# A hybrid decoder layer on one core: the compressed attention's normalisation and the choice of blocks become two steps on VectorE

## The reference

```python
# for each block of 128 queries
s = q @ k_cmp.T * scale - slope * dist          # 63 compressed keys
p_cmp = softmax(masked s) * ok
o_cmp = p_cmp @ v_cmp
imp = (p_cmp summed over heads) @ overlap       # importance of 32 blocks
score = where(ok_sel, where(forced, 1e4, imp), -1)
idx = top_k(score, 4)                           # blocks chosen per token
o_sel = attention over the chosen blocks
o_win = attention over a window of 512
o_a = g0 * o_cmp + g1 * o_sel + g2 * o_win
...
merged = sigmoid(m0) * (o_a @ w_br_nsa) + sigmoid(m1) * (o_b @ w_br_s5)
       + sigmoid(m2) * (o_c @ w_br_sb)          # m0, m1, m2 = h @ columns of w_in
```

## Time and profile before

| | |
|---|---|
| median of three runs | 1378.1 us |
| the profiled execution: its time, its span | 1379.38 us, 1377.6 us |
| TensorE matmuls busy | 1314.1 us (95%) |
| VectorE, GpSimd, ScalarE busy | 795.0, 603.8, 517.6 us |
| chain that ended last: TensorE, VectorE | 87%, 7% of the span |

### The profile page before, as it was taken

The page is one execution under the profiler, slowest core; times in us unless marked ns, Lnnn a source line. Parts: engine busy times, 40 slices in busy tenths (PEclk is TensorE's granted clock), DMA queues, the critical chain, the costliest instruction groups (busy, mean ns, idle before and its releaser), DMA issues.

```text
span 1377.6 us, 18689 instructions
## 1 busy us (share of the span) xinstructions
PE 1314.1 (95%) x7157; PEld 1059.5 (77%) x7157; DVE 795.0 (58%) x1289; ACT 517.6 (38%) x990; POOL 603.8 (44%) x395
## 2 busy tenths in 40 slices
PE   6999898999999889999989999999999999999998
PEld 5888565789787667666778888878888888888887
DVE  5895676632625867667636341287444543479952
ACT  6322553400122255555511010265545554463441
POOL 4213003134542310111148746267776777757662
PEclk9999999999999989999999999999999999999999
DMA  7530100032201210000155524151222211156343
GB/s 195 49 56 20 46 1 19 29 63 58 59 20 39 86 45 9 24 24 5 45 181 191 202 94 181 39 176 46 88 77 74 62 54 54 47 185 199 115 113 146
DMA packets 143673, 110.75 MB, mean 80 GB/s; under 512 B 41936, under 2 KB 116048, under 8 KB 143568
## 3 DMA queue, kind: packets, MB, share of 16 engines
q1 hardware_dynamic: 142784, 107.98, 26.8%
q10 hardware_dynamic: 800, 1.57, 0.5%
HBM read 86.33 MB, written 21.63 MB: 78 GB/s over the span
## 4 chain that ended last, share of the span: by engine, by line
PE 87%; DVE 7%; ACT 3%; issue 2%; DMA 0%; SPq 0%; ACTq 0%; DVEq 0%
PE ps L964 24%; PE ps L966 23%; PE ps L965 23%; PE ps L1506 2%; PE ps L1490 2%; PE ps L1222 1%; PE ps L1239 1%; PE ps L1471 1%; PE ps L1252 1%; DVE merged L2304 1%; PE ps L1473 1%; DVE hTl L2062 1%; PE ps L1083 1%; PE ps L1422 1%; PE ps L1196 0%
## 5 line engine op out<-in xcount | busy, mean ns | idle before, releaser
L964 PE MATMUL ps<-hTh,wh 128*128 128x512 f32 x784 | 314.8, 402 | 3.1 <-DVE hTl L2062 2.3
L966 PE MATMUL ps<-hTh,wl 128*128 128x512 f32 x784 | 306.2, 391 | 0.0
L965 PE MATMUL ps<-hTl,wh 128*128 128x512 f32 x784 | 306.0, 390 | 0.0
L924 POOL TENSOR_TENSOR wl<-raw,wh 128x512 fp32r<-128x512 f32 x162 | 235.2, 1458 | 154.7 <-ACT wh L1901 154.7
L828 POOL TENSOR_TENSOR wh<-raw,zero 128x1280 fp32r<-128x1280 f32 (+2 forms) x36 | 79.9, 2220 | 474.1 <-PE ps L966 470.1
L964 PEld LDWEIGHTS ps<-hTh,wh 128*128 128x128 f32 x784 | 148.0, 189 | 38.1 <-issue 8.0
L831 POOL TENSOR_TENSOR wl<-raw,wh 128x1280 fp32r<-128x1280 f32 (+2 forms) x45 | 129.7, 2881 | 105.4 <-ACT wh L1661 102.6
L964 PE MATMUL ps<-wh,hTh 128*128 128x512 f32 (+2 forms) x496 | 173.1, 349 | 0.0
L966 PE MATMUL ps<-wh,hTl 128*128 128x512 f32 (+2 forms) x496 | 173.0, 349 | 0.0
L965 PE MATMUL ps<-wl,hTh 128*128 128x512 f32 (+2 forms) x496 | 172.8, 348 | 0.0
L966 PEld LDWEIGHTS ps<-hTh,wl 128*128 128x128 f32 x784 | 147.4, 188 | 32.1
(11 more groups left out here) (377 smaller groups left out, 2338.6 us busy)
## 6 DMA issues: line engine op xcount, KB each, us to landing
raw<-in_w_in SPq DMA_DIRECT2D x35, 512.0 KB, 3.9
raw<-in_w_up SPq DMA_DIRECT2D x64, 256.0 KB, 2.8
arena<-in_w_down SPq DMA_DIRECT2D x32, 256.0 KB, 3.7
v_down<-arena SPq DMA_DIRECT2D x32, 256.0 KB, 2.6
raw<-v_down SPq DMA_DIRECT2D x32, 256.0 KB, 2.7
raw<-in_w_down SPq DMA_DIRECT2D x24, 256.0 KB, 2.9
merged<-in_x SPq DMA_DIRECT2D x8, 512.0 KB, 6.5
raw<-in_w_out SPq DMA_DIRECT2D x8, 512.0 KB, 3.7
```

The costliest lines, as they stand in the source:

```text
L924: eng.tensor_tensor(wlf[:, w_slot(n)], raw_piece(n), whf[:, w_slot(n)].bitcast(F32), ALU.subtract).then_inc(S("fw_split"), 1)
L964: mm(out_, ah, bh, start=first, stop=False, skip_group_check=True)
L965: mm(out_, ah, bl, start=False, stop=False, skip_group_check=True)
L966: return mm(out_, al, bh, start=False, stop=last, skip_group_check=True)
```

## The change

Three things, all in the order of steps; no instruction is added or taken away.

- `select_blocks` is cut in two functions: `normalise` (to `pc_ready`) is what `soft` calls now, `select_blocks` (the rest) is the new step `select`.
- First half: `select` 0 stands three pieces later than `soft` 0, after piece 24, so that VectorE's merge (8, 0) comes between the two parts. Second half: `select` 1 stands after piece 49, so that both `ka` steps and merge (10, 1) come between.
- Second half on TensorE: `pc` 4 and `pc` 5 stand after piece 50 instead of 53, and `pvc` 4 to 6, `pc` 6 and 7 come three pieces sooner too; `pvc` 7 and `qa` 0 two, `mk` 1 and `qa` 1 one; on VectorE, `qa` 0 now comes ahead of merge (11, 0).

```diff
-        PLAN += F(13) + [("half", 0), ("half_exp", 0)] + F(14, 20) + [("split", 0)] + F(20, 22) + [("soft", 0)] + F(22, 37)
+        PLAN += F(13) + [("half", 0), ("half_exp", 0)] + F(14, 20) + [("split", 0)] + F(20, 22) + [("soft", 0)] + F(22, 25) + [("select", 0)] + F(25, 37)
...
-        PLAN += [("ka", 0), ("ka", 1)] + F(48, 51) + [("kb", 0), ("kb", 1)] + F(51, 54)
-        PLAN += [("pc", 4), ("pc", 5)] + F(54) + [("pvc", 4), ("pc", 6)] + F(55) + [("pvc", 5), ("pc", 7), ("qa", 0)] + F(56)
-        PLAN += [("pvc", 6), ("mk", 1), ("pvc", 7), ("qb", 0)] + F(57, 59) + [("qa", 1)] + F(59, 61) + [("qb", 1)]
+        PLAN += [("ka", 0), ("ka", 1)] + F(48, 50) + [("select", 1)] + F(50) + [("kb", 0), ("kb", 1), ("pc", 4), ("pc", 5)]
+        PLAN += F(51) + [("pvc", 4), ("pc", 6)] + F(52) + [("pvc", 5), ("pc", 7)] + F(53) + [("pvc", 6), ("qa", 0)] + F(54)
+        PLAN += [("pvc", 7), ("qb", 0)] + F(55) + [("mk", 1)] + F(56, 58) + [("qa", 1)] + F(58, 61) + [("qb", 1)]
...
-            def select_blocks(hb):
+            def normalise(hb):
...
                 ins.then_inc(S("pc_ready"), 1)
+
+            def select_blocks(hb):
+
                 then(tt(imp, php[:, :, 0:64:2], php[:, :, 2:66:2], ALU.add))
...
                 elif kind == "soft":
+                    normalise(n)
+                elif kind == "select":
                     select_blocks(n)
```

## The result

| | before | after |
|---|---|---|
| median, us | 1378.1 (5 runs, 1376.68 to 1379.85) | 1369.89 (5 runs, 1367.68 to 1372.0) |
| ratio to before | | 0.9936, 95% interval 0.9925 to 0.9947 |
| profiled execution: its time, its span | 1379.38, 1377.6 | 1367.76, 1366.0 |

The change makes the kernel 0.64% faster, some 8.8 us (7.3 to 10.3). The forecast was 1368.4 in a range from 1366.0 to 1373.0.

What follows compares the result with a forecast made beforehand. TensorE's matmuls were busy 95% of the span, so only its idle and low-clock time could be won. 3.4 + 6.2 = 9.6 us off 1379.38 gives 1369.8; off the median, less one tenth, 1368.4, range 1366.0 to 1373.0.

Steps and rivals of the forecast that it cites:

- the two waits: TensorE waits on L2301 before pieces 29 (2.80 us) and 54 (5.42 us), claimed to come from VectorE's order, not its speed.
- First half, 3.4 us: Moving select 0 behind merge (8, 0) wins 4.4 us at piece 29, less about 1.0 waited at piece 34.
- the race at the end of L828: On VectorE, whether L2473 or GpSimd's L831 starts first around 431.15: first half wins 4.4 or 3.4 us; 3.4 taken.
- rival 1: L2473 slips in ahead of L831 or isn't held: first half 4.4 us, total 10.6, so 1367.5; chance 0.27.
- the signs that the prediction named: In the first half's selection, L2472 lasts about 0.9 us and L2473 either 0.23 or about 3.
- Second half, 6.2 us: Wait before piece 54 (5.42 us) and its low clock (2.6) go, less a wait of 1.75 before pc 4.
- The new wait: In the second half, TensorE waits 1.75 us before pc 4 for pc_ready, ended by L2459, with no clock loss.
- the store: Third row of merged lands 3.8 us after L2304, at 479.4; ScalarE's qa 0 waits, TensorE keeps 4.9 us of cover.
- Rival 3: Something unseen sets the main loop's start, and the second half's gain is waited away: 3.4 us left, 1374.7; chance 0.08.
- Rival 4: A slow store landing delays qa 0 and merge (11, 0) behind it; a landing of 20 us gives 1380; chance 0.02.
- rival 2: The clock falls at piece 34, pc 4 or both, each costing up to 1.5 us: 1370 to 1371.5; chance 0.18.
- The shift is kept to the end: After 500 us nothing is bound to an absolute time, so the 9.6 us won should last to the end.

Runs made afterwards that it cites:

- pc_only: Changed kernel, but select 1 called right behind soft 1, TensorE's new order kept; mean 1370.9 us, ratio 0.9941 to the kernel before.
- first_only: Kernel before with only the first half changed (select 0 after piece 24); mean 1374.4 us, ratio 0.9967 to the kernel before.
- after_again: The changed kernel itself, timed once more without any edit; mean 1369.2 us.
- both: Changed kernel with select 0 after piece 29, and pc 4, 5 and what follows up to mk 1 one piece later; mean 1370.2 us over 11 runs.
- select_only: Changed kernel, but TensorE's second half in the old order (pc 4 and 5 after piece 53); mean 1372.4 us, ratio 0.9947 to the kernel before.

## Why the prediction was right

**Bound, and the two waits.** Right: both waits on L2301 came from VectorE's order. (In the second half they could be met on TensorE's side as well, as pc_only shows.) The merge ahead of the selection started exactly where the selection had; piece 29 waited for nothing (L2301 ended at 425.71, the piece began at 426.02), and the low clock at 430 us was gone.

**First half, 3.4 us.** Measured 3.3 (piece 34 at 434.00 instead of 438.40, less the 1.1 us by which all was earlier) and 3.2 in first_only. That the selection would run into GpSimd's split and piece 34 pay for it was right, and so was the size (wait 0.95, worked out as 1.0). One step failed in its detail: I had the first tensor_scalar held by L828 and the second by L831. It was the copy of 16 columns, which I had not thought of as such an instruction, that L828 held, and the first tensor_scalar that L831 held. Each takes the place of the other, so the sum didn't change, and the race at the end of L828, on which rival 1 hung, didn't take place: the copy ended at 430.01, L831 began at 430.06, and 0.8 us of `match_replace` lay between the copy and the next one that could be blocked. So the signs that the prediction named, L2472 at 0.9 us and L2473 at 0.23 or about 3, were not the ones seen (2.25 and 0.23), and that 3.4 came out and not 4.4 was in part luck: the reason given for it, the lost race, was not the one at work. The rule of the Trainium skill (SBUF — State Buffer, "Who interferes with whom"), that copy and tensor_scalar in the two-port mode contend with GpSimd and the later one blocks entirely, agrees with 1.85, 2.25 and, with L828 away, 0.17 us.

**Second half, 6.2 us.** Measured 6.2 alone and in the change. The new wait was 1.54 for 1.75 worked out; `ka` held by L831 and the merge in time were as forecast, and so was the store: ScalarE waited 0.90 us for it and VectorE's `qa` 0 0.68 us for ScalarE, but TensorE waited for neither.

**The other queues, rivals 3 and 4.** Rival 3 fell: the stage up to the first L1471 is 9.4 us shorter, and the loop behind it is no longer than before (202.0 for 202.6). Merge (11, 0) behind `qa` 0 was read at 476.5, 5.6 us ahead of piece 59 (482.11). Rival 4 is not decided by experiment: the store was never slowed down.

**Clock, rival 2.** Neither new wait lowered the clock; the mean granted clock of the stage was 1.00, in after_again too. But the argument for that was weak: I took the earlier trace rows to show that a wait of 1.77 us leaves the clock alone. The same wait, in "both", did lower it, and 2.22 us in select_only did. The row was one draw.

**The shift is kept to the end.** This is the step whose size was off. In the profiled execution it was kept (loop 202.0 for 202.6). In the median it was not quite: 8.2 us instead of 9.7, and the slowest of the five runs, 1372.0, had a clock of 0.986 where the fastest, 1367.68, had 0.990. A different draw in the main loop moves a single execution by 5 us or more (loops of 202.0 and 207.1 us here; 1364.05 and 1371.99 us for the one program of "both"), more than half of what the change is worth. The prediction had no term for this, only "one us of luck" at the fast end of its range; its reason, that nothing behind 500 us is bound to an absolute time, says nothing on the clock. That job's difference of the means is 8.3 and after_again's 9.4, so the 1.5 us between forecast and median are no more than the runs scatter.

## What to carry to other kernels

When an in-order engine runs a long chain of small steps, cut it at each signal and put what TensorE waits for next between the parts; then look once more at what has come to stand behind the second part. A short copy, tensor_scalar or tensor_tensor within SBUF costs VectorE 0.16 to 0.3 us here until it falls beside a long GpSimd instruction: then it takes as long as what is left of that, so put it where nobody waits. A gain of under 0.5% in a kernel with clock dips is to be read stage by stage in the trace; the total carries a draw of the clock behind it.

## What the runs showed of the hardware

- A copy of 128 x 16 float32 within SBUF took 0.17 us where no GpSimd instruction was under way, and 1.85 us when issued 0.5 us after one of 2.32 us had begun. A tensor_tensor of 128 x 1 took 0.16 us, and 2.29 us when issued 1.0 us after a GpSimd instruction of 3.26 us had begun.
- The same wait of 1.77 us, followed by 0.68, on the same stretch of work left the granted clock at 1.00 in one kernel and at 0.66 (mean over 10 us) in another; the executions of "both" had a mean clock over the whole span from 0.984 (1371 to 1372 us) to 0.991 (1364 us), without any change in the program.
